# A state-space scan inside a two-model kernel: step and skip products taken from PSUM, one decay product a head, and the pooling branch moved ahead

## The reference, cut to what matters

```
u, z, xbc, dt = split(x @ w_in)                  # 512, 1024, 1536, 16 columns
y_pool = einsum(mean_w(u) - u, pool_w) * pool_scale
xs, bm, cm = split(silu(causal_dwconv(xbc)))
dt = softplus(dt + dt_bias);  xdt = xh * dtc;  acs = cumsum(dt * a)
lmat = exp(where(tri, acs[l] - acs[s], -inf))    # per head
y_diag = einsum('bcgls,bcgels,bcsgep->bclgep', cb, lmat, xdt)
states = einsum('bclgn,bcgel,bclgep->bcgepn', bc, decay_states, xdt)
y = y_diag + y_off + xh * d_skip
y = rms_norm(y * silu(z));  out = concat(y_pool, y) @ w_out
```

## Time and profile before

| | |
|---|---|
| median of 3 timed runs | 2491.43 us (2489.44 to 2493.94) |
| the profiled execution: time, span | 2483.87 us, 2481.7 us |
| mean granted PE clock over the span | 0.992 of full |
| PE busy, share of the span | 2430.3 us, 98% |
| DVE, ACT, POOL busy | 29%, 38%, 44% |

### The profile page before, as it was taken

How to read it: one execution, slowest core, us unless ns; L and a number is a source line. 1 busy time by engine, 2 the same in 40 slices (tenths; PEclk the granted TensorE clock), 3 DMA queues, 4 the chain that set the end, 5 groups by cost and what they waited for, 6 DMA issues and landing times.

```text
span 2481.7 us, 29800 instructions
## 1 busy us (share of the span) xinstructions
PE 2430.3 (98%) x11691; PEld 1984.9 (80%) x11691; DVE 724.7 (29%) x1289; ACT 946.1 (38%) x1896; POOL 1088.6 (44%) x893
## 2 busy tenths in 40 slices
PE   8999999999999999999999999999999999999998
PEld 7867888887867888887885788888888767888887
DVE  2233420223374320214244441010152464210104
ACT  4523442433474432433444333323233553332231
POOL 4523544444403544454544444444454402544443
PEclk9999999999999999999998999999999999999999
DMA  5312333332202333332320233333233201433332
GB/s 174 85 51 64 91 97 98 98 98 81 77 27 80 96 97 98 98 97 90 106 81 26 81 103 97 98 98 97 86 101 86 69 1 60 124 98 98 98 97 74
DMA packets 161395, 215.62 MB, mean 87 GB/s; under 512 B 38199, under 2 KB 86095, under 8 KB 161255
## 3 DMA queue, kind: packets, MB, share of 16 engines
q1 hardware_dynamic: 157632, 203.65, 27.4%
q10 hardware_dynamic: 3623, 10.07, 1.3%
HBM read 211.00 MB, written 2.10 MB: 86 GB/s over the span
## 4 chain that ended last, share of the span: by engine, by line
PE 92%; DVE 4%; POOL 2%; ACT 1%; issue 1%; DMA 0%; ACTq 0%; DVEq 0%; POOLq 0%
PE PS L333 14%; PE PS L335 14%; PE PS L334 14%; PE PS L339 13%; PE PS L341 13%; PE PS L340 13%; PE PS L1364 3%; PE PS L1347 1%; PE PS L414 1%; PE PS L2138 1%; POOL WL L306 1%; PE PS L2130 1%; DVE X L654 1%; PE PS L993 1%; PE PS L1466 0%
## 5 line engine op out<-in xcount | busy, mean ns | idle before, releaser
L306 POOL TENSOR_TENSOR WL<-WS,WH 128x512 fp32r<-128x512 f32 (+2 forms) x788 | 1004.5, 1282 | 1221.0 <-ACT WH L299 1216.9
L299 ACT ACTIVATE WH<-WS 128x512 fp32r<-128x512 f32 (+2 forms) x788 | 479.6, 615 | 1237.8 <-PE PS L341 631.1
L333 PE MATMUL PS<-AH,WH 128*128 128x512 f32 (+1 forms) x1712 | 641.3, 375 | 4.1 <-DVE AL L449 2.9
L334 PE MATMUL PS<-AL,WH 128*128 128x512 f32 (+1 forms) x1712 | 638.3, 373 | 0.0
L335 PE MATMUL PS<-AH,WL 128*128 128x512 f32 (+1 forms) x1712 | 638.2, 373 | 0.0
L333 PEld LDWEIGHTS PS<-AH,WH 128*128 128x128 f32 x1712 | 325.6, 190 | 62.7 <-issue 6.6
L334 PEld LDWEIGHTS PS<-AL,WH 128*128 128x128 f32 x1712 | 325.5, 190 | 55.5 <-issue 0.5
L335 PEld LDWEIGHTS PS<-AH,WL 128*128 128x128 f32 x1712 | 325.3, 190 | 55.6
L341 PE MATMUL PS<-WH,h_HL 128*128 128x512 f32 x864 | 336.1, 389 | 0.0
L339 PE MATMUL PS<-WH,h_HH 128*128 128x512 f32 x864 | 336.1, 389 | 0.0
L340 PE MATMUL PS<-WL,h_HH 128*128 128x512 f32 x864 | 336.1, 389 | 0.0
(11 more groups left out here) (315 smaller groups left out, 2018.6 us busy)
## 6 DMA issues: line engine op xcount, KB each, us to landing
WS<-in_mlp_w_up_dram SPq DMA_DIRECT2D x128, 256.0 KB, 2.8
WS<-in_mlp_w_down_dram SPq DMA_DIRECT2D x128, 256.0 KB, 2.6
WS<-in_ffn_w_gate_dram SPq DMA_DIRECT2D x176, 128.0 KB, 2.1
WS<-in_ffn_w_up_dram SPq DMA_DIRECT2D x176, 128.0 KB, 2.2
WS<-in_ffn_w_down_dram SPq DMA_DIRECT2D x88, 256.0 KB, 2.6
WS<-in_gla_w_in_dram SPq DMA_DIRECT2D x48, 256.0 KB, 2.7
WS<-in_even_w_in_dram SPq DMA_DIRECT2D x48, 256.0 KB, 2.7
WS<-in_odd_w_in_dram SPq DMA_DIRECT2D x32, 256.0 KB, 2.7
```

The source lines that it names most:

```text
L299: e.activation(WH[:, s, 0:n], WS[:, s, 0:n], ACT.Copy).then_inc(hi.sem, hi.tick(i))
L306: e.tensor_tensor(WL[:, s, 0:n], WS[:, s, 0:n], WH[:, s, 0:n].bitcast(F32), ALU.subtract).then_inc(lo.sem, lo.tick(i))
L333: e.matmul(o, h, xh[:, cs], start=start, stop=False, skip_group_check=free)
L334: e.matmul(o, h, xl[:, cs], start=False, stop=False, skip_group_check=free)
```

## The change

Five edits, all in the even mixer:

1. DVE's copy of each `xs` piece becomes two products out of the same bank: `x * dt` into `eXS`, and `x * d_skip` into `ACC`. The bank is free after the second. POOL's seven skip products (eight tiles' worth, two groups of four) go, and POOL's `decayed` loses DVE's `dd` factor.
2. With `dt` in `eXS`, DVE's four products a head become one `tensor_tensor` of 512 columns.
3. The stationary and moving operands of the exponents' matmul grow from 48 to 96 rows; rows 48 to 95 are zero.
4. The pooling branch moves from `ev.z1` to `ev.bc` on PE, ACT and DVE; `products` and ACT's copies of `eCB` move from step 6 of `ev.z1` to step 3.
5. `decayed` of group 1 writes into `eBAND`, free by then, and moves with the rest ahead of the scan.

```diff
-        PAIR = sb("PAIR", [48, 16], F32R)
+        PAIR = sb("PAIR", [96, 16], F32R)
-        eAR = take("AR", [48, T], F32R)
+        eAR = take("AR", [96, T], F32R)
-        eXE = at("e_XE", al_off, [P, 3, T])
-        eTM = at("e_TM", al_off + 3 * T * 4, [P, 2, T])
+        eXE = eBAND[:, :, :].rearrange("p (t a) n -> p t (a n)", t=3)
+        eTM = at("e_TM", al_off, [P, 2, T])
...
+            for kc in gemm(e, w, "ev.bc", "F", cols(ew, 2560, 512), 8, AHL, eB, feats("mlp1"), held):
+                if kc == 2:
+                    pool_mean(0)
+                    pool_mean(1)
+                elif kc == 3:
+                    pool_mix(0)
+                    pool_mix(1)
+                    pool_mean(2)
+                    pool_mean(3)
+                elif kc == 4:
+                    pool_mix(2)
+                    pool_mix(3)
...
-                held[b] = (ve, "xs", c)
+                held[b] = (ve, "skip", c)
...
             for kc in gemm(e, w, "ev.z1", "T", cols(ew, 1024, 512), 8, AHL, eB, feats("mlp1"), held):
-                if kc == 0:
-                    pool_mean(0)
-                    pool_mean(1)
-                elif kc == 1:
+                if kc == 1:
                     decay_rows()
-                elif kc == 2:
-                    pool_mix(0)
-                    pool_mix(1)
                 elif kc == 3:
-                    pool_mean(2)
-                    pool_mean(3)
-                elif kc == 5:
-                    pool_mix(2)
-                    pool_mix(3)
-                elif kc == 6:
                     products(0)
                     products(1)
...
-                    e.matmul(PS[b][:, :], PAIR[:, u:u + 1].broadcast_to((48, P)), eAR[:, :], start=True, stop=False,
+                    e.matmul(PS[b][:, :], PAIR[:, u:u + 1].broadcast_to((96, P)), eAR[:, :], start=True, stop=False,
...
-            e.activation(eAR[0:32, :], CK[0:32, 0:T], ACT.Copy, scale=0.0).then_inc(sc.sem, sc.tick("rows0"))
+            e.activation(eAR[:, :], CK[0:96, 0:T], ACT.Copy, scale=0.0).then_inc(sc.sem, sc.tick("rows0"))
...
-            w.wait_ge(sc, "e5")
-            e.tensor_tensor(DTF[4], DTF[4], DTF[0], ALU.mult).then_inc(ve.sem, ve.tick("dd"))
...
-                e.tensor_copy(eXS[:, :, c * P:(c + 1) * P], PS[conv_bank(c)][:, :].rearrange("p (t n) -> p t n", t=NT)).then_inc(
-                    ve.sem, ve.tick("xs", c))
+                e.tensor_tensor(pair(eXS[:, :, cs]), p4, dt, ALU.mult).then_inc(ve.sem, ve.tick("xs", c))
+                e.tensor_tensor(pair(ACC[g][:, :, (c % 4) * P:(c % 4 + 1) * P]), p4, dsk, ALU.mult).then_inc(
+                    ve.sem, ve.tick("skip", c))
...
-                    for t in range(NT):
-                        e.scalar_tensor_tensor(eM[:, u % 3, t, :], eL[:, u % 3, t, :], DT[0][:, t, u:u + 1], eCB[:, g, t, :],
-                                               ALU.mult, ALU.mult).then_inc(ve.sem, ve.tick("m", u))
+                    e.tensor_tensor(eM[:, u % 3, :, :], eL[:, u % 3, :, :], eCB[:, g, :, :], ALU.mult).then_inc(
+                        ve.sem, ve.tick("m", u))
...
             for kc in weight_steps(weight_lo, e, w, "ev.z1", 8):
-                if kc == 1:
+                if kc in (0, 2):
                     for t in range(3):
-                        decayed(t, 0)
-                        skip(t, 0)
-                    skip(3, 0)
+                        decayed(t, kc // 2)
```

More of the change, by code:

```diff
@@ L1150, in dve_gla @@
             dve_feat(e, w, "n0", 1, BA, V_MIXPRE, [])
-            e.tensor_tensor(PAIR[:, :], CK[0:48, C_ID:C_ID + 16], CK[0:48, C_ID + 32:C_ID + 48], ALU.add).then_inc(
+            e.tensor_tensor(PAIR[:, :], CK[0:96, C_ID:C_ID + 16], CK[0:96, C_ID + 32:C_ID + 48], ALU.add).then_inc(
                 ve.sem, ve.tick("pair"))
@@ L1604, in acc_in @@
         def acc_in(g, t):
-            return (ve, "acc", g, t) if t else (po, "skip", g, 0)
+            return (ve, "acc", g, t) if t else (ve, "skip", 4 * g + 3)
         def pe_even(e, w, held):
@@ L1611, in pe_even, with pool_mean, pool_mix @@
                 held[eA[t]] = (ve, "u", t)
-            run(gemm(e, w, "ev.bc", "F", cols(ew, 2560, 512), 8, AHL, eB, feats("mlp1"), held))
+            def pool_mean(g):
+                b, gs = eA[g], slice(g * P, (g + 1) * P)
+                w.wait_ge(*held[b])
+                w.wait_ge(ld["bands"], 0)
+                w.wait_ge(ve, "u", 3)
+                for t in range(NT):
+                    o = PS[b][:, t * P:(t + 1) * P]
+                    q = e.matmul(o, U[:, t, gs], eBAND[:, 3 * g + (1 if t else 0), :], start=True, stop=t == 0)
+                    if t:
+                        q = e.matmul(o, U[:, t - 1, gs], eBAND[:, 3 * g + 2, :], start=False, stop=True)
+                q.then_inc(mm.sem, mm.tick("mean", g))
+            def pool_mix(g):
+                b = eA[g]
+                w.wait_ge(ve, "mean", g)
+                e.matmul(PS[b][:, :], ePW[:, g, :], eDF[:, g % 2, :], start=True, stop=True).then_inc(
+                    mm.sem, mm.tick("mix", g))
+                held[b] = (ve, "mix", g)
+            for kc in gemm(e, w, "ev.bc", "F", cols(ew, 2560, 512), 8, AHL, eB, feats("mlp1"), held):
[10 more added lines that the diff above has]
+                    pool_mix(3)
             for m in range(4):
@@ L1804, in act_even, with pool_mix @@
             run(weight_steps(weight_hi, e, w, "ev.u", 8))
-            run(weight_steps(weight_hi, e, w, "ev.bc", 8))
+            def pool_mix(g):
+                w.wait_ge(mm, "mix", g)
+                e.activation(ePH[:, g, :], PS[eA[g]][:, :], ACT.Copy, scale=vcol(V_PSC + g)).then_inc(
+                    sc.sem, sc.tick("mix", g))
+            for kc in weight_steps(weight_hi, e, w, "ev.bc", 8):
+                if kc in (3, 4):
+                    pool_mix(2 * kc - 6)
+                    pool_mix(2 * kc - 5)
             def taps(c):
@@ L1911, in dve_even, with pool_mean, pool_mix @@
                 e.tensor_copy(U[:, t, :], PS[eA[t]][:, :]).then_inc(ve.sem, ve.tick("u", t))
+            def pool_mean(g):
+                w.wait_ge(mm, "mean", g)
+                if g > 1:
+                    w.wait_ge(mm, "mix", g - 2)
+                e.tensor_copy(eDF[:, g % 2, :], PS[eA[g]][:, :]).then_inc(ve.sem, ve.tick("mean", g))
+            def pool_mix(g):
+                w.wait_ge(sc, "mix", g)
+                e.scalar_tensor_tensor(ePL[:, g, :], PS[eA[g]][:, :], vcol(V_PSC + g), ePH[:, g, :].bitcast(F32), ALU.mult,
+                                       ALU.subtract).then_inc(ve.sem, ve.tick("mix", g))
+            for g in (0, 2):
+                pool_mean(g)
+                pool_mean(g + 1)
+                pool_mix(g)
+                pool_mix(g + 1)
             def taps(c):
@@ L1959, in dve_even @@
                     xs_tokens(4 * g + m)
[L1961 to L1972, removed]
             w.wait_ge(sc, "rows")
@@ L2059, in decayed @@
                 w.wait_ge(ve, "xs", 4 * g + 3)
[L2060 removed]
+                w.wait_ge(sc, "e4")
                 w.wait_ge(mm, "xs", 7)
[L2062 to L2063 removed]
                 e.tensor_tensor(heads(xe_buf(t, g)), heads(eXS[:, t, g * T:(g + 1) * T]), per_head(4, t, g), ALU.mult).then_inc(
                     po.sem, po.tick("xe", g, t))
[L2067 to L2073 removed]
             for kc in weight_steps(weight_lo, e, w, "ev.z1", 8):
[L2075 removed]
+                if kc in (0, 2):
                     for t in range(3):
[L2077 to L2079 removed]
+                        decayed(t, kc // 2)
             def decay_state(t, g):
@@ L2091, in gate @@
                 e.tensor_tensor(Y[:, t, gs], Y[:, t, gs], ACC[g][:, t, :], ALU.mult).then_inc(po.sem, po.tick("yz", g, t))
-            for u in range(10):
-                if u % 8 in (1, 3):
-                    decay_state(u % 8 // 2 + 1, u // 8)
-                if u in (2, 4, 6):
-                    decayed(u // 2 - 1, 1)
-                if u in (4, 6):
-                    skip(u // 2 - 1, 1)
-                elif u == 7:
-                    skip(0, 1)
-                    skip(3, 1)
+            decay_state(1, 0)
+            decay_state(2, 0)
+            decay_state(1, 1)
             for t in range(NT):
```

29 lines of the change are left out of this document (7 added, 22 removed).

## The result

| | before | change |
|---|---|---|
| median of the timed runs | 2491.34 us (2489.44 to 2493.94) | 2475.03 us (2473.85 to 2478.66) |
| ratio, 95% interval | | 0.9936 [0.9919, 0.9954] |
| the profiled execution: time, span, clock | 2483.87, 2481.7, 0.992 | 2475.68, 2473.9, 0.994 |
| scan, first `state_in` to the start of the last `y` matmul | 52.3 us | 42.8 us |

The two profiled executions differ by only 8.2. The first comparison to make is therefore between the two profiles, and the second question is why the medians lie twice as far apart.

A forecast was written before the change was run, and what follows sets the result against it. PE was taken as the bound, with waits and half-clock stretches in the scan. Rows 3.2 + product waits 1.6 + clock 3.4 + banks' sum 0.6 - given back 1.0 = 7.8 us, so 2483.6 us; range 2479.5 to 2489.0.

The forecast's parts named there:

- the last of the sum: Whole run: 7.8 us, all gained in the scan, taken off the timed median of 2491.43 to give 2483.6.
- Rows, 3.2: Scan, exponents' matmul: with 96 rows the mask loads ahead, 0.43 becomes 0.23 a head, 3.2 us over 16 heads.
- The clock, 3.4: Scan, heads 3 to 7: without the 1.28 us wait the middle 6.8 us stretch stays at 2.4 GHz, 3.4 us.
- the third stretch: Scan, last of three stretches at 1.2 GHz, 6.8 us long: no gain counted, a faster PE would wait for ACT's squares.
- the wait for the sum: Scan, head 8: DVE's add that frees the `y` banks comes earlier, some 1.3 us instead of 1.92, gaining 0.6.
- the clock holds through: Rival, scan: the first stretch at 1.2 GHz goes too, and part of the third; gain 9.5 to 12 us, chance 0.17.
- Waits, 1.6 + 0.6 - 1.0 = 1.2: Scan: 1.6 from product waits of 0.36 and 1.28, 0.6 from the banks' sum, less 1.0 lost behind ACT's squares.
- The wait at head 12 behind ACT: Scan, sign: a faster PE reaches head 12's exponents before ACT frees head 10's bank, losing 1.0 us.
- given back: Scan, heads 8 to 12: PE's gain of 0.2 a head is lost behind ACT's squares, 1.0 us.
- The cost kept for a decay beside the new product: Scan, heads 8 and 9: a POOL state decay could hold a DVE product; 0 taken, 1.1 us kept for the range.
- Counted at nothing: Ahead of the scan: moved pooling branch, larger zero fill and `xs` products, 0 each; at risk 1.6 us at `ev.z0`.
- The slower case: Rival, scan: more idle PE leaves the chip at 1.2 GHz longer; 4 us more, time 2495, chance 0.06.

The follow-up runs named there:

- The two kernels with the wait filled: Before and the change, each with eight useless mask matmuls in PE's 1.88 us wait ahead of the odd mixer's attention: 2485.92 and 2475.38 us.
- the shift of 0.9 us: Kernel before with transposes repeated in the odd mixer, so PE reaches the attention's wait some 0.9 us later: 2486.99 us, ratio 0.9997.
- before, 96 rows: Kernel before with only the exponents' matmul grown from 48 to 96 rows: 2485.50 us, ratio 0.9979.
- the other order: The change with ACT's squares of group 0 behind head 12 instead of 9 and DVE's adds ahead of head 9's product: 2472.12 us; 2473.50 with the attention's wait filled.
- POOL's work alone: The change with seven POOL products back in the scan, four of them into a tile nothing reads: 2475.14 us, ratio 0.9952.

## Why the prediction was wrong

**The step that failed** is the last of the sum: "the median of the timed runs is 7.6 us above it, and 2491.43 - 7.8 = 2483.6". It carried the gap between profile and median of before over to the change as a constant. The gap is a mechanism of its own: a stretch at 1.2 GHz in the odd mixer's attention, worth 7.7 us, which the profiled execution of before lacks. Of 15 timed executions of the change 11 are under 2479, and its median lies 0.6 below its profiled execution. The two kernels with the wait filled split the gain: 10.5 us remain, and the rest of the 16.3, 5.8, goes with the filling. That the executions of 2490 us or more come by the wait ahead of the attention is shown by filling it. That this stretch is what they lose is inferred: its 7.7 us are the gap, their clock is lower, and the stretch was seen in profiles of five kernels (one of them the change unaltered), though in neither of the two of before unaltered, both of which are among its faster executions. Why before has the stretch oftener than the change stays open: the wait of 1.88 and the work around it are the same in both, only 8 us earlier, and the shift of 0.9 us gave no answer.

**Profile against profile** the sum was near: 9.5 us in the scan where 7.8 was forecast, and 42.8 us where 44.6 was. Of the 9.5, 8.2 reached the time; the scan begins 0.4 later and the same work between it and the odd attention takes 1.2 more. There the change has a stretch of 3.4 us at a granted clock of 0.51, from 1381.5 to 1384.9, that before lacks. Its third profile has such a stretch too; its second has none there and takes 581.8 us for that work, as before does.

**Rows, 3.2.** A head fell by 0.23, 16 x 0.23 = 3.7. The price was near and its place half right. The exponents' matmul gives the mask way after 1360.79 - 1360.47 = 0.32 instead of 0.43, not after 0.23. The mask's load is still not ahead of its matmul (0.15 idle, 1360.78 against 1360.79). The other 0.12 lies in `y`, which gives way after 1361.83 - 1361.02 = 0.81 instead of 0.93; the exponents' load now starts at 1360.44, 0.03 ahead of its matmul. The load's own time hardly depends on the rows, 0.19 for 96 and 0.18 for 48; without this term the sum would have been 3.7 too small in the matmuls, and the two filled kernels with 48 and 96 rows lie 6.0 apart in time.

**The clock, 3.4.** This is the mis-sized term of the sum. Within the profile pair it is 8.0 - 3.2 = 4.8, since the third stretch halved as well. I had counted nothing for it because "a faster PE would only wait longer for the squares"; it didn't, as the wait for the sum is now in three pieces of 1.29, 0.16 and 0.16. (The third stretch of before did not follow its wait either: it starts at 1355.3, inside the 1.92 us that end at 1356.27.) Over the executions it is larger: profiles of the kernel before and its variants with 48 rows have 17.1 to 30.7 us of the scan at half clock, those of the change 3.4 to 6.8. Half of the difference is 5 to 14 us. The case "the clock holds through" was nearer, with its 9.5 to 12, though the first stretch, which it wanted gone, stayed in the first profile. 3.7 and 4.8 are the whole of PE's 8.5.

**Waits, 1.6 + 0.6 - 1.0 = 1.2.** Idle time fell by 1.1, for partly other reasons. The waits of 0.36 and 1.28 went, as said, and 0.48 before the last head became 0.23. The wait for the sum became 1.6 in total, 0.3 gained where 0.6 was forecast. Not foreseen: 0.65 for the bank that ACT's copy of `z` holds, and 1.02 instead of 0.74 for the first exponential; both are also in "before, 96 rows", so they come from a PE that arrives earlier. The wait at head 12 behind ACT didn't show; the time is lost in the 0.91 for the state just before it. That something was given back is borne out by the other order: at the same 3.4 us of half clock its two scans take 40.6 and 40.3 us, where the change's take 41.3 in both profiles.

**The product, and POOL.** 0.69 a head as forecast. With four pieces alone the scan is 43.5 and the longest wait for a product 0.3; with POOL's work alone it is 44.1 and a wait of 0.92 is back; both together bring waits of 1.17 and 1.11. So the 1.28 went by POOL's work, as forecast, and the single product without that would have taken only a part of it. The cost kept for a decay beside the new product was not tested: none of the 16 products lasts over 693 ns, but no decay of the profile lies beside one for more than 0.1 us. Two of DVE's adds with both inputs in SBUF did meet one and lasted 0.91 and 0.88 instead of 0.69. DVE's and POOL's timelines of the change:

```profile
1333.43 0.91 DVE L2005 TENSOR_TENSOR eg_ACC<-eg_ACC,e_TM 128x512 f32<-128x512 f32 x1
1332.75 1.04 POOL L2076 TENSOR_TENSOR JUNK<-JUNK,e_DT 128x512 f32<-128x512 f32 x1 [6.10 <-PE PS L1751]
```

**Counted at nothing.** The products out of PSUM take 0.68 to 0.69, not 1.14 in four pieces, and PE has no wait at `ev.z0`. The zero fill and the earlier pooling branch cost nothing to be seen in the part ahead of the scan. The branch alone in the kernel before is 0.14% slower, inside the 0.2% that a measurement of this kernel can tell.

**The slower case** was seen as a mechanism, in the wrong kernel: a single stretch of 27.3 us at 1.2 GHz stands in two profiles of the kernel before with small edits, and in none of the change.

## What to carry to other kernels

Before a forecast is taken off a median, ask which of the timed executions the profile shows: where profile and median differ by 0.3%, the difference may be a stage that the change never touches. A second profile of the same kernel may not show it, as here; the mean granted clock of the timed executions did, and profiles of close variants showed the place. Count what a removed wait does to the clock behind it by all stretches, and take their length from more than one execution. A wait of PE that can't be removed can be filled with useless matmuls: worth 6.2 us here ahead of the attention, a long dense part, and nothing in the scan's shorter waits.

## What the runs showed of the hardware

- Behind one and the same wait of 1.88 us PE runs its attention at 2.4 GHz in two profiles of the change and at 1.2 GHz for 17.1 us in a third. The 17.1 us cost 7.7.
- With 1.8 us of mask matmuls in that wait none of 12 executions of before reaches 2490 us, where 72 of 98 without them do.
- A stretch at 1.2 GHz can last 27.3 us while PE is busy for 26.34 of them.
- DVE operations with both inputs in SBUF take longer beside POOL's products: 3.48 instead of 1.14 us for four pieces, up to 1.58 instead of 0.69 for one product.
- A matmul with a stationary operand of 48 rows hands over later than one of 96 with rows of zeros: 1.59 against 1.36 us for the group of exponents, mask and `y`, though twice the rows are loaded.
- DVE's product of a PSUM tile with a step size broadcast along each head's columns takes 0.69 us, as a plain one does.
